# Rotary row swaps: by transfers instead of matmuls, and another order of two steps on VectorE

## What is computed

```python
def partial_rope(t, positions):            # t: (B, S, H, 2, d)
    half = ROT_DIM // 2                    # 8
    inv_freq = ROPE_THETA ** (-jnp.arange(0, ROT_DIM, 2) / ROT_DIM)
    ang = positions[..., None] * inv_freq
    cos, sin = jnp.cos(ang)..., jnp.sin(ang)...
    t1, t2, rest = tf[..., :half], tf[..., half:ROT_DIM], tf[..., ROT_DIM:]
    return jnp.concatenate([t1 * cos - t2 * sin, t2 * cos + t1 * sin, rest], axis=-1)

q, k, v, u = h @ w_in                      # q, k: 4 heads x 2 x 64
q, k = partial_rope(q, pos), partial_rope(k, pos)
p = softmax(mask(q @ k.T * scale))         # for both halves
a = (p[:, :, 0] - lam * p[:, :, 1]) @ v    # then a norm for each head
c = silu(layernorm(causal_dwconv(u1 * sigmoid(u2))))   # 31 taps, 512 channels
y = concat([a, c]) @ w_out                 # then cross attention and a convolution FFN
```

## Time and profile before

| | us |
|---|---|
| median of 3 runs | 1303.47 (1302.02 to 1304.37) |
| the profiled execution | 1301.79 |
| its span, first to last instruction | 1300.0 |
| TensorE busy | 1258.9 (97%) |
| VectorE busy | 757.2 (58%) |
| GpSimd busy | 747.1 (57%) |
| ScalarE busy | 585.0 (45%) |

### The profile page before, as it was taken

The page is one execution under the profiler, slowest core; times in us unless marked ns, Lnnn a source line. Parts: engine busy times, 40 slices in busy tenths (PEclk is TensorE's granted clock), DMA queues, the critical chain, the costliest instruction groups (busy, mean ns, idle before and its releaser), DMA issues.

```text
span 1300.0 us, 16886 instructions
## 1 busy us (share of the span) xinstructions
PE 1258.9 (97%) x6162; PEld 1047.0 (81%) x6162; DVE 757.2 (58%) x1233; ACT 585.0 (45%) x951; POOL 747.1 (57%) x862
## 2 busy tenths in 40 slices
PE   5989999999999999999999999999999999999997
PEld 4868878878888888887778988888888888888885
DVE  5857788434434367699687427655457616651564
ACT  3366566456655346233456645434333313331341
POOL 2643543433343676676445869534659857885782
PEclk9989999999999999999999999999999999999998
DMA  9421224232334743232214443222313333223221
GB/s 380 168 82 57 81 81 140 96 98 93 110 115 135 242 128 99 81 98 89 61 69 154 131 163 114 81 66 65 93 55 112 100 112 97 97 98 98 97 81 65
DMA packets 41698, 142.46 MB, mean 110 GB/s; under 512 B 4624, under 2 KB 5136, under 8 KB 40464
## 3 DMA queue, kind: packets, MB, share of 16 engines
q1 hardware_dynamic: 41616, 141.39, 32.7%
HBM read 130.88 MB, written 8.39 MB: 107 GB/s over the span
## 4 chain that ended last, share of the span: by engine, by line
PE 70%; DVE 19%; ACT 6%; issue 2%; POOL 1%; DMA 1%; SPq 0%; DVEq 0%; ACTq 0%; POOLq 0%
PE ps L124 69%; DVE tm L137 4%; DVE ac L137 3%; ACT tm L131 3%; DVE tm L134 2%; ACT L131 1%; PE ps L128 1%; DVE x L137 1%; POOL wl L134 1%; DVE ewl L134 1%; DVE spl L134 1%; ACT wh L131 1%; DVE zh L145 1%; DMA x<-xin 1%; DVE ewh L145 1%
## 5 line engine op out<-in xcount | busy, mean ns | idle before, releaser
L134 POOL TENSOR_TENSOR wl<-raw,wh 128x256 fp32r<-128x256 f32 x804 | 690.7, 890 | 496.6 <-ACT wh L131 488.7
L131 ACT ACTIVATE wh<-raw 128x1024 fp32r<-128x1024 f32 x201 | 212.2, 1056 | 319.3 <-PE ps L124 308.2
L124 PE MATMUL ps<-hh,wh 128*128 128x512 f32 x872 | 344.1, 395 | 0.0
L124 PE MATMUL ps<-hh,wl 128*128 128x512 f32 x872 | 340.5, 391 | 0.0
L124 PE MATMUL ps<-hl,wh 128*128 128x512 f32 x872 | 340.3, 390 | 0.0
L124 PEld LDWEIGHTS ps<-hh,wl 128*128 128x128 f32 x872 | 164.1, 188 | 35.1
L124 PEld LDWEIGHTS ps<-hh,wh 128*128 128x128 f32 x872 | 164.2, 188 | 33.3 <-DVE tm L137 0.4
L124 PEld LDWEIGHTS ps<-hl,wh 128*128 128x128 f32 x872 | 164.3, 188 | 33.0
L134 DVE TENSOR_TENSOR tm<-tm,tm 128x512 f32<-128x512 f32 (+3 forms) x110 | 90.7, 829 | 46.5 <-ACT tm L131 43.6
L137 DVE SCALAR_TENSOR_TENSOR tm<-cb,par_sb,tm 128x512 f32<-128x512 f32 x88 | 87.4, 993 | 50.9 <-ACT tm L131 47.5
L131 ACT ACTIVATE tm<-tm 128x512 f32<-128x512 f32 (+3 forms) x109 | 53.8, 530 | 83.8 <-DVE tm L137 67.8
(11 more groups left out here) (305 smaller groups left out, 2281.4 us busy)
## 6 DMA issues: line engine op xcount, KB each, us to landing
raw<-units SPq DMA_DIRECT2D x201, 512.0 KB, 3.5
ada<-units SPq DMA_DIRECT2D x16, 512.0 KB, 14.6
kept<-ge SPq DMA_DIRECT2D x16, 256.0 KB, 2.8
tm<-kept SPq DMA_DIRECT2D x16, 256.0 KB, 3.7
tm<-gate_w SPq DMA_DIRECT2D x12, 256.0 KB, 3.9
x<-xin SPq DMA_DIRECT2D x2, 1024.0 KB, 6.2
x<-xin SPq DMA_DIRECT2D x1, 2048.0 KB, 10.9
out<-x SPq DMA_DIRECT2D x8, 256.0 KB, 2.2
```

The source lines that it names most:

```text
L124: return self.none if self.e is None else self.e.matmul(out, lhs, rhs, start=start, stop=stop, skip_group_check=skip)
L131: return self.none if self.e is None else self.e.activation(out, in_, func, **kw)
L134: return self.none if self.e is None else self.e.tensor_tensor(out, a, b, op)
```

## The change

The rotation's two matmuls, the constant `rot` and the low part `RTl` go. ScalarE's copy of the bank goes to `RX` in full fp32, and the rows are exchanged by four transfers from `RX` to a tile `RS` (8 rows of 512 elements each), at the end of each projection: ScalarE issues them, behind the refill of the ring, for seven of the eight, SyncE for the keys of head 3, ahead of the transfers that bring back the memory. All other rows of `RS` are zeroed once by GpSimd. The sign moves into the table of angles. VectorE's cosine product no longer has a subtraction ahead of it; the sine product reads `RS` and waits for the landing (`l_rot`); bank 0 is free after the cosine product. On VectorE, at the steps with keys (n = 1, 5, 9), `turn_d(n)` now comes ahead of `dproj(h, 5)`. The transfers of one projection wait for the sine product of the one before.

```diff
-CONSTS = ["tri8", "m8", "o1024", "o128", "o512", "rot", "ident", "triu", "one"]
-N_R = 6
+CONSTS = ["tri8", "m8", "o1024", "o128", "o512", "ident", "triu", "one"]
+N_R = 5
...
-        out[g:g + 8, o + 8] = inv
+        out[g:g + 8, o + 8] = -inv
...
-    RTh = at("rth", [P, T], F32R)
-    RTl = at("rtl", [P, T], F32R)
+    RX = at("rx", [P, T], F32)
+    RS = at("rs", [P, T], F32)
...
         def dproj(h, step):
             b, nm = 0, ("dq", "dk")[step // 3]
-            if step % 3 < 2:
-                hhalf("m", (nm, h), step % 3, b)
-                return
-            pe.wait_ge(s_rl, nm, h)
-            pe.wait_ge(s_rx, nm, h, 1)
-            pe.mm(PS[b][:, :], con_r("rot"), RTh[:, :], True, False)
-            pe.mm(PS[b][:, :], con_r("rot"), RTl[:, :], False, True).then_inc(*s_rot.up(nm, h))
-            bank[b] = (s_rx, (nm, h, 2))
+            hhalf("m", (nm, h), step % 3, b)
+            if step % 3:
+                bank[b] = (s_rx, (nm, h, 1))
...
+    def turned_rows(e, nm, h):
+        n = d_order.index((nm, h))
+        e.wait_ge(s_rh, nm, h)
+        if n:
+            e.wait_ge(s_rx, *d_order[n - 1], 2)
+        else:
+            e.wait_ge(s_pad, 3)
+        for x, o in enumerate((0, 8, 64, 72)):
+            e.dma(RS[o:o + 8, :], RX[o ^ 8:(o ^ 8) + 8, :]).then_inc(*l_rot.up(nm, h, x))
...
             if n:
-                act.wait_ge(s_rot, *d_order[n - 1])
-            act.fn(RTh[:, :], PS[b][:, :], ACT.Copy).then_inc(*s_rh.up(nm, h))
+                act.wait_ge(l_rot, *d_order[n - 1], 3)
+            act.fn(RX[:, :], PS[b][:, :], ACT.Copy).then_inc(*s_rh.up(nm, h))
             refill((nm, h))
+            if (nm, h) != ("dk", 3):
+                turned_rows(act, nm, h)
...
                 dve.wait_ge(s_rh, nm, h)
-                split_low(RTl[:, :], PS[b][:, :], RTh[:, :], (nm, h), s_rl)
                 dve.wait_ge(s_tab, "st")
                 dve.stt(TM[5][:, :], PS[b][:, :], q_scale(nm), CT[:, :], ALU.mult, ALU.mult).then_inc(*s_rx.up(nm, h, 1))
             if step % 3 == 2:
-                dve.wait_ge(s_rot, nm, h)
-                dve.stt(TM[6][:, :], PS[b][:, :], q_scale(nm), STb[:, :], ALU.mult, ALU.mult).then_inc(*s_rx.up(nm, h, 2))
+                dve.wait_ge(l_rot, nm, h, 3)
+                dve.stt(TM[6][:, :], RS[:, :], q_scale(nm), STb[:, :], ALU.mult, ALU.mult).then_inc(*s_rx.up(nm, h, 2))
...
-            if step == 4:
-                dproj(h, 5)
             turn_d(n)
-            if step == 1:
-                dproj(h, 2)
+            if step in (1, 4):
+                dproj(h, step + 1)
...
+        pool.zero(RS[:, :]).then_inc(*s_pad.up(3))
...
             if j == PLACE["dk", 3] + 2 * RING:
                 sp.wait_ge(s_unit, ("dk", 3))
+                turned_rows(sp, "dk", 3)
                 for x, t in enumerate((MTh, MTl)):
```

More of the change, by code:

```diff
@@ L55, in constants @@
     }
-    rot = np.zeros((128, 128))
-    for g in (0, 64):
-        for j in range(8):
-            rot[g + 8 + j, g + j] = -1.0
-            rot[g + j, g + 8 + j] = 1.0
-    c["rot"] = rot
     out = np.zeros((128, NCON), np.float32)
@@ L428, in build @@
         sig(n) for n in ("s_ux", "s_us", "s_cp", "s_cph", "s_cpl", "s_pad", "s_tap", "s_ac"))
-    s_rh, s_rl, s_rx, s_rot, s_dh, s_dl, s_yf = (
-        sig(n) for n in ("s_rh", "s_rl", "s_rx", "s_rot", "s_dh", "s_dl", "s_yf"))
+    s_rh, s_rx, s_dh, s_dl, s_yf = sig("s_rh"), sig("s_rx"), sig("s_dh"), sig("s_dl"), sig("s_yf")
+    l_rot = sig("l_rot", 16)
     s_lnp, s_lnd, s_lny, s_lna, s_ych, s_ycl, s_sub, s_ydh, s_ydl = (
@@ L1012, in tensor_program @@
         conv(0)
-        dproj(0, 2)
         conv(1)
@@ L1017, in tensor_program @@
         conv(2)
-        dproj(0, 5)
         conv(3)
@@ L1023, in tensor_program @@
         qk_d(1)
-        dproj(1, 2)
         for n in range(16):
@@ L1249, in q_scale @@
         return 0.125 if br in ("b", "dq") else 1.0
+    d_order = [(nm, h) for h in range(4) for nm in ("dq", "dk")]
+    def turned_rows(e, nm, h):
[7 more added lines that the diff above has]
+            e.dma(RS[o:o + 8, :], RX[o ^ 8:(o ^ 8) + 8, :]).then_inc(*l_rot.up(nm, h, x))
     def cq_bank(f):
@@ L1541, in conv_out @@
                 act.fn(AC[j][:, :], PS[1][:, :], ACT.Identity, bias=pcol("cv_dw_b_2", j)).then_inc(*s_ac.up(j))
-        d_order = [(nm, h) for h in range(4) for nm in ("dq", "dk")]
         def dproj(h, step):
```

## The result

| | before | after |
|---|---|---|
| median of 7 runs each, us | 1302.02 (1301.49 to 1304.37) | 1306.32 (1305.65 to 1307.55) |
| ratio of after to before, 95% interval | | 1.0029 [1.0020, 1.0039] |
| the profiled execution, us | 1301.79 | 1305.96 |
| its span, us | 1300.0 | 1304.2 |
| granted clock, mean of that execution | 0.991 | 0.987 |

The change makes the kernel 4.3 us slower. I had forecast 3.9 us faster and a range that ends at 1303.5.

A forecast was written before the change was run, and what follows sets the result against it. TensorE, busy 97% of the span, bounds the kernel; 8.2 us of matmuls and waits saved, less 4.45 of new waits, with 0.1 for first matmuls, made 3.9 us: 1303.47 to 1299.6 us, range 1296.0 to 1303.5.

The forecast's parts named there:

- the prelude: Ahead of the loop: TensorE is spared rotation matmuls and waits of 1.2 us (first query) and 0.6 us (second query).
- The wait for dkl at n = 1: Keys of head 1: low part done at 635.9 us, TensorE at qk_d(4) at 635.5, a new wait of 0.4 us.
- four cost 0 to 1.3 us: Issuing each projection's four transfers holds the queue 0 to 1.3 us, from 0.33 us at least per issue.
- 0.95 more than that: Keys of head 3 (n = 9): kv(0, 0) begins 0.95 us later than now, counted from the projection's end.
- L: Time from the end of the RX copy to the last landing: 2.2 to 4.8 us, taken as 3.5.
- the rows land late: Rival: VectorE's wait for landing holds up what follows; over 0.2% slower from L of 6.4 us; chance 0.12.
- waits 0.55 us: Keys of head 2 (n = 5): low part done at 667.75 us, so TensorE waits 0.55 us at qk_d(8).
- The new order as a gain: n = 1, 5, 9: turn_d ahead of the keys' rotation removes TensorE's waits for atl, 0.23, 0.3 and 1.68 us.
- so no cost here is the clock's: Differential attention, 585 to 765 us: granted clock 1.00 throughout in the kernel before, so the clock costs nothing.
- slower: Rival: over 0.2% slower, only by rows landing late; at L = 7, 5.5 us slower, 1309; chance 0.12.
- within 0.2%: Rival: the gain is spread into VectorE's waits, leaving 2.0 us at L = 5, 1301.5 us; chance 0.28.

The follow-up runs named there:

- e2: The changed kernel with VectorE's old order (keys' rotation ahead of turn_d at n = 1, 5, 9), transfers kept; 1303.90 us, ratio 1.0004 to the kernel before.
- e7: The changed kernel with ScalarE, not SyncE, issuing the transfers of head 3's keys, so SyncE issues the memory loads at once; 1308.00 us, ratio 1.0031.
- e1: The kernel before with only VectorE's order changed (turn_d ahead of the keys' rotation at n = 1, 5, 9), rotation still by matmuls; 1306.44 us, ratio 1.0028.
- e3: The changed kernel plus 15 matmuls nobody reads at n = 10: 9 ahead of qk_d(12), 6 ahead of kv(0, 0); 1303.67 us, ratio 1.0001.
- e5: The changed kernel with VectorE's old order and 16 matmuls nobody reads ahead of pv_d(4) at n = 10; 1301.43 us, ratio 0.9982.
- e6: The changed kernel with VectorE's old order and the keys of heads 1, 2 and 3 rotated by matmuls; 1300.15 us, ratio 0.9971.
- e4: The changed kernel with only the keys of head 3 rotated by matmuls, no transfers on SyncE for them, new order kept; 1301.20 us, ratio 0.9984.
- e8: The changed kernel with two transfers instead of four per projection, so half of each head is rotated wrongly; 1305.22 us, ratio 1.0010.
- e9: The changed kernel, old order, keys of heads 1 to 3 by matmuls, 7 unread matmuls ahead of pv_d(4), 4 ahead of sub_sum(2); 1296.97 us, ratio 0.9953.
- e12: The kernel before with VectorE's new order, plus unread matmuls: 6 ahead of qk_d(12), 4 ahead of sub_sum(2); 1305.81 us, ratio 1.0020.

## Why the prediction was wrong

What was right: no rth, no rtl, 16 matmuls fewer; the first idle time gone; the prelude, where I had 3.2 us by my terms (six matmuls 1.4, waits 1.2 and 0.6) and all kernels with its transfers show 3.75; landings covered at the first query and keys; atl ahead of the sine product at n = 1, 5, 9; the sine product inside its bounds at 0.68 us in the median and 0.75 on average, less than the 0.9 that I took (the bound of 1.3 was nearly reached once, with 1.22); and that TensorE, once past the stage, keeps what it has. The wait for dkl at n = 1, 0.4 us forecast and 0.41 measured, was luck: the rotation took 3.4 us there instead of 2.9, and TensorE came later too, held 0.56 us by a wait for ac at 629.25 us that I did not have.

By the shifts the forecast missed by 7.5 us (-3.9 against +3.64). About 2.0 of them had arisen by 690 us, where my terms give -4.7 us (prelude, eight more matmuls, waits) and -2.67 was measured; 2.3 arose between there and kv(0, 0); 3.1 are the clock's behind it. What failed, in the order of the sum:

1. *"four cost 0 to 1.3 us".* The term of the issues was mis-sized: 2.6 us on ScalarE, 2.86 on SyncE. I scaled from an issue of 128 rows (0.33 us, the least in the trace; the mtl that the earlier trace rows shows took 0.43) and took that for an upper bound of a smaller one; 0.63 us was measured. Over 1.3 us for four issues was one of my own signs of being wrong. At n = 9 it also delayed the loads: mtl went out 4.6 us behind the projection's end where I had 2.8 (1.5 of the difference are the issues, 0.3 the square that sub_sum reads, which stood ahead of the RX copy on ScalarE). kv(0, 0) began 11.9 us behind the end of that projection (688.9 to 700.83); before it was 8.7 (690.8 to 699.55), and I had 0.95 more than that. That is 2.3 us of the miss.

2. *"I take L = 3.5".* L was 4.0 us on ScalarE's queue and 4.3 on SyncE's (4.8 in e2), of which 2.0 behind the last issue's start. Within my bounds, at their upper part, and short of the 6.4 us that my rival "the rows land late" asked for. The lateness came from the queue, not from the landing. With the memory loads beside it, L did reach 7.7 (e7).

3. *n = 5: "waits 0.55 us".* 1.41 us were measured. The rotation there took 3.4 us, not 2.7 (cast 0.84 and low part 1.09 us, where the kernel before took 0.43 and 0.69; the four low parts of keys average 1.00 us). Also the wait for rt ahead of sub_sum at that step grew from 0.3 to 1.3 us: TensorE came earlier and ScalarE did not. I had not priced a wait that was already there and becomes longer because its engine arrives sooner, nor one, as for ac at n = 1, that comes up for that reason. The two waits for dkl in the changed kernel:

```profile
633.38 0.33 PE L118 MATMUL ps<-dkh,dqh 64*128 64x128 f32 x2 [0.41 <-DVE dkl L128]
...
666.51 0.33 PE L118 MATMUL ps<-dkh,dqh 64*128 64x128 f32 x2 [1.41 <-DVE dkl L128]
```

Why the rotation took longer at n = 5 the trace shows. GpSimd, then VectorE in the changed kernel:

```profile
663.74 3.95 POOL L128 TENSOR_TENSOR wl<-raw,wh 128x256 fp32r<-128x256 f32 x4 [1.46 <-ACT wh L125]
...
665.32 1.09 DVE L128 TENSOR_TENSOR dkl<-tm,dkh 128x512 fp32r<-128x512 f32 x1
```

The cast and the low part fell into GpSimd's four subtractions for the next unit. In the kernel before they fell into its pause (664.37 to 666.42 us) and took 0.43 and 0.69 us. It is so at all eight low parts of keys in the two kernels: 1.09 to 1.11 us where a subtraction of GpSimd was under way when they began, 0.69 where none was. I had taken the shorter rotation for n = 5 and the longer for n = 9 (2.6 us measured, beside no GpSimd).

4. *The new order as a gain.* I counted 0.23 + 0.3 + 1.68 us for the waits for atl, and put the rotation's stay behind ath at n = 1 and 5 against it at 0.95 us. Alone (e1) the order costs 3.7 us, with the transfers 2.5 (e3 against e5, whose fills differ). It does not only exchange one wait for another: it lets VectorE stand idle with the rotation ready, for 1.18 us at n = 5 and as long at n = 9; at n = 5 the later rotation falls beside GpSimd's subtractions (cast 0.84, low part 1.09 us, as above); and dkl, which TensorE needs as soon as it has atl, is the longer chain.

5. *"so no cost here is the clock's".* The clock was a term put at nothing. It was read from a column that describes one execution of the kernel before and used for a kernel with other idle times. In the changed kernel TensorE is idle for over 5 us of 691 to 701, the clock falls to its lower level there and once more behind 727 us, and 3.1 us more are lost while TensorE has work (e3: filled, they come back). The rival "slower" had only transfers as its mechanism; none of my cases had this one. Without it the changed kernel would have been at +0.3 to +0.5 us by the shifts: within 0.2%.

The sum by what was measured, in the profile's shifts: 3.75 us won ahead of the loop, 1.1 lost up to 690 us; 3.2 lost from there to kv(0, 0) (waits of 0.61, 2.37, 0.54 and 1.54 us against 0.42 and 1.68 before, less the 0.47 us of two matmuls: 2.5; part of the rest is the clock's already, since turn_d's three matmuls take 0.90 us instead of 0.50); 3.1 lost to the clock: -3.75 + 1.1 + 3.2 + 3.1 = +3.65 us, where I had -3.9.

By the ratios, on the way from the changed kernel to the best one: filling its idle time returns 3.6 us (1.0029 to 1.0001), the old order 2.5 (to 0.9982), the keys of the loop by matmul 3.8 (to 0.9953).

What stays open: why the same idle time lowers the clock in one kernel and not in another (e6 and the kernel before at pv_d(4); e4 and the changed kernel at sub_sum(0); e7 and the changed kernel ahead of qk_d(8)). Ahead of sub_sum(2) all of before, the changed kernel and e1 to e8 wait 1.1 us; the clock fell there in those six profiles (the changed kernel, e1, e2, e6, e7, e8) in which it had also fallen between 694 and 704 us, and in none of the others (before, e3, e4, e5). Why is not shown. Open is also why two transfers instead of four shorten the delay of the rows by 0.5 to 0.8 us and not by 1.3. Whether the old order would still be better at n = 9 with only the rows late was not tried by itself.

## What to carry to other kernels

To move work off a busy engine onto transfers pays where other work covers issue and landing (here 4 us; ahead of the loop and for the queries), and loses where TensorE waits at the end of a chain that starts with the landing. Count issues by what a transfer of that shape costs its queue, and everything behind them in that queue. An engine that reaches its next wait earlier gains nothing there; ask of each place what is then late, and on a busy TensorE price the idle time twice, once as itself and once as the clock behind it. Before putting ready work behind a wait to serve another consumer, compare both chains to that consumer: the shorter one may wait, the longer one may not.

## What the runs showed of the hardware

- A transfer of 8 rows by 2 KB from SBUF to SBUF holds ScalarE's or SyncE's queue for 0.63 us (the first 1.22), against 0.33 us for a load of 128 rows by 4 KB. ScalarE's arithmetic queued ahead of it runs on meanwhile (the refill copy of 1.05 us), what is behind it does not start.
- The last of four lands 2.0 us behind the start of its issue with no memory load ahead of it, the last of two 2.85 us (e8), and the last of four 5.7 us beside 2 MB of loads issued 2 us before from another queue (e7).
- TensorE's granted clock fell from 1.00 to 0.50 behind idle times of 0.71 and 1.28 us (e4), 1.41 (e7), 1.68 (e6) and 2.37 (the changed kernel), and did not behind equal ones: 1.68 in the kernel before, 1.27 and 1.41 in the changed kernel, all at the same places of the program. Behind the 1.13 us ahead of sub_sum(2) it fell in six profiles and not in four. A fall cost about 1.5 us where TensorE had work. With useless matmuls in the idle time the clock was 1.00 in this stage in every profile (e3, e5, e9 to e12).
- The sine product from two SBUF tiles took 0.68 us in the median, no more than from PSUM. In the changed kernel it took 1.22 us at head 0's keys, where a subtraction of GpSimd was under way when it began (602.27 to 603.46 us, product from 602.78), and 0.68 to 0.69 us at the seven others, where none was. In e8 it was the same: 0.95 to 1.22 us at the three places with such a subtraction under way, 0.68 at the five others.
